# First weight chunk in two halves on one queue, dummy products ahead of the first transposes, and products that wait for half of a transposed tile

## The chip, the cores and the metric

The kernel runs on one core of one Trainium2 chip. The metric is device time in microseconds (us) of one execution: the median over several runs. The core has a matrix engine (TensorE, PE in the profile; its weight loads are listed apart as PEld), VectorE (DVE), ScalarE (ACT), GpSimd (POOL) and SyncE (SP). SP and ACT each have a queue on which they issue transfers between the chip's main memory and the core's on-chip memory; matrix products land in eight banks of an accumulator memory, from which ScalarE and VectorE copy them.

## The reference

One sequence of 256 tokens, model width 1024, all in 32-bit floating point, goes through two kinds of block:

```python
# first_block, two layers
proj = x @ ab_w_in[0]                       # 1024 -> 2840
o    = concat([nsa_attention(...), moba_attention(...)])
x    = layer_norm(ALPHA * x + o @ ab_w_out[0], ...)
x    = layer_norm(ALPHA * x + grouped_moe(x, ...), ...)
q, k, v = split(x @ sb_w_in[0])             # the second mixer
x    = layer_norm(ALPHA * x + mixer(q, k, v) @ sb_w_out[0], ...)
x    = layer_norm(ALPHA * x + grouped_moe(x, ...), ...)
# second_block, one layer
u    = rmsnorm(x) ; proj = u @ w_in_2[0]    # 1024 -> 3104
x    = x + concat([gla_mixer(...), dilated_mixer(...)]) @ w_out_2[0]
u    = rmsnorm(x) ; x = x + hier_moe(u, ...)
out  = rmsnorm(x)
```

The names of the mixers are shortened here; each starts with a projection of the whole normalised input, and each mixture of experts (MoE) starts with a router, a narrow product of the same input.

## The kernel before

The 256 tokens are two tiles of 128 (T = 2), the width of 1024 is eight steps of 128 (KT = 8). Products need the tokens along the free dimension, so ahead of every projection and every router the input is transposed by TensorE into four banks: bank 2t holds steps 0 to 3 of tile t, bank 2t + 1 steps 4 to 7. ScalarE copies banks 0, 1 and 2 into `XT` (L1574, semaphore `xt_act`), VectorE bank 3 (L1884, `xt_dve`). This happens six times, k = 0 to 5: k = 0 for x itself, k = 1, 3 and 5 ahead of the three routers, k = 2 ahead of the second mixer's projection, k = 4 ahead of the second block's.

All the code is written out by hand for each engine; each engine works through its own list in order, and semaphores tie them together. `transpose_x` (L728) issues the transposes of tile 0, then, where it is given, the work `then(0)` behind a wait for both copies of tile 0, then the transposes of tile 1, the filler `between`, and `then(1)` behind a wait for both copies of tile 1. The first call (L904) has no `then`: the products of chunk 0 follow it. The waits for tile t of the normalised input (`normed`) stand ahead of its transposes; VectorE computes the two tiles one after the other.

Weights come in chunks of 2 MB (1024 x 512) into six slots. A chunk's load is issued by SP when TensorE has finished with the chunk six places before it (`chunk_done`); TensorE waits for `slot_loaded`. `project` (L761) multiplies a chunk with both tiles, 16 products of 128x128 by 128x512; each is two instructions in the profile. The first chunk is loaded in two halves of the contraction, steps 0 to 3 by SP (L655) behind x, and steps 4 to 7 by ACT (L1561) behind the first 80 KB of constants, among which is the identity matrix that transposes need; both halves count on the semaphore of slot 0. The small loads of ACT's queue (positions, two small weights, two tables of position embeddings) stand behind its half, and the 1.5 MB of further constants (L1605) behind ScalarE's copies of the first transposes.

`keep_clock_up` (L746) issues products whose results nobody reads, to fill waiting time of TensorE. In the MoEs, `logits` (L1033) is the `then` of `transpose_x`; it is the router's product, and behind it VectorE chooses the experts. The first chunk of the second mixer is `N_SB`, at L1347; the first chunk of the second block `N_2`, at L1426. In both, `then(t)` is `project` for one tile.

## Time and profile before

| | before |
|---|---|
| time, median of 3 runs | 1242.79 us (1242.15 to 1244.42) |
| the profiled execution | 1239.27 us, its span 1237.4 us |
| TensorE busy | 93% of the span |
| TensorE's weight loads, VectorE, ScalarE | 46%, 26%, 17% |
| loaded and stored | 364.41 MB, mean 295 GB/s |

The profile is one execution, recorded by the hardware. Times in it are counted from the span's start. Matrix instructions are pipelined, so the end of a group of them is some 0.2 us after the time at which the next may start.

### The profile page before, as it was taken

How to read it: one execution, taken by the hardware profiler on the slowest of the kernel's cores; microseconds unless marked ns; L12 is line 12 of the kernel's file. 1: busy time of each engine (PE TensorE's matmuls, PEld its weight loads, DVE VectorE, ACT ScalarE, POOL GpSimd, SP SyncE). 2: the span in 40 equal slices, each digit the busy share in tenths (PEclk: the TensorE clock that was granted, in tenths of full speed). 3: DMA queues.
4: the chain of work that ended last, by engine and by line, in shares of the span. 5: the costliest groups of instructions: out<-in, count | busy, mean ns of one | idle time of the engine just before them, and what ended most of it. 6: DMA issues, size and time to landing. Idle time of an engine off the chain costs nothing.

```text
span 1237.4 us, 14481 instructions
## 1 busy us (share of the span) xinstructions
PE 1155.5 (93%) x5884; PEld 565.1 (46%) x5884; DVE 316.2 (26%) x898; ACT 207.6 (17%) x474; POOL 1.0 (0%) x6
## 2 busy tenths in 40 slices
PE   7999999999999999999899999989987998989995
PEld 3555555554687546554364545422422242233231
DVE  1466362112113343111513665100010010000002
ACT  2135321111024412111113231100000000000001
POOL 0000000000000000000000000000000000000000
PEclk9999999999999999999999999999999999999998
DMA  9794135999833133999763244799999999999994
GB/s 311 166 266 180 69 136 243 405 417 390 311 137 136 69 136 130 406 418 389 274 221 136 72 151 186 281 427 426 428 427 429 427 426 430 428 429 426 429 426 185
DMA packets 78250, 364.41 MB, mean 295 GB/s; under 512 B 21458, under 2 KB 26868, under 8 KB 53620
## 3 DMA queue, kind: packets, MB, share of 16 engines
q1 hardware_dynamic: 76724, 360.88, 74.0%
q10 hardware_dynamic: 1472, 2.78, 0.6%
q8 instruction: 38, 0.62, 0.2%
q14 instruction: 16, 0.13, 0.0%
HBM read 362.60 MB, written 1.05 MB: 294 GB/s over the span
## 4 chain that ended last, share of the span: by engine, by line
PE 75%; DMA 15%; DVE 6%; issue 2%; ACT 1%; SPq 0%; ACTq 0%; DVEq 0%
PE bank L1139 17%; DMA weights<-in_expert_w_down_dram 14%; PE bank L1195 9%; PE bank L797 8%; PE bank L819 7%; PE bank L1177 5%; PE bank L769 5%; PE bank L784 4%; PE bank L1232 3%; PE bank L1084 2%; PE bank L809 2%; PE bank L1087 2%; PE bank L847 1%; PE bank L887 1%; PE bank L1372 1%
## 5 line engine op out<-in xcount | busy, mean ns | idle before, releaser
L1139 PE MATMUL bank<-weights,projected 128*64 128x256 f32 (+1 forms) x2048 | 341.1, 489 | 17.3 <-DMA weights<-in_expert_w_up_dram 6.6
L1139 PEld LDWEIGHTS bank<-weights,projected 128*64 128x64 f32 (+1 forms) x2048 | 133.3, 124 | 209.7 <-issue 169.2
L1195 PE MATMUL bank<-weights,work 128*32 128x512 f32 x448 | 106.8, 632 | 23.4 <-DMA weights<-in_expert_w_down_dram 23.4
L797 PE MATMUL bank<-weights,x_transposed 128*128 128x512 f32 x256 | 118.6, 602 | 0.9 <-ACT heads_transposed L1629 0.9
L819 PE MATMUL bank<-weights,mixed 128*128 128x512 f32 x192 | 86.9, 599 | 1.6 <-DVE mixed L2086 1.1
L1195 PEld LDWEIGHTS bank<-weights,work 128*32 128x32 f32 x448 | 30.1, 115 | 97.7 <-issue 97.7
L769 PE MATMUL bank<-weights,x_transposed 128*128 128x512 f32 (+1 forms) x160 | 64.0, 557 | 4.8 <-ACT x_transposed L1574 3.3
L2278 DVE COPY work<-bank 64x512 f32<-64x512 f32 (+1 forms) x30 | 20.7, 689 | 184.8 <-PE bank L1195 125.3
L797 PEld LDWEIGHTS bank<-weights,x_transposed 128*128 128x128 f32 x256 | 45.7, 190 | 47.3 <-issue 45.4
L2298 DVE TENSOR_TENSOR work<-work,bank 64x512 f32<-64x512 f32 (+1 forms) x24 | 16.4, 682 | 199.0 <-PE bank L1139 199.0
L1715 ACT ACTIVATE work<-bank 128x512 f32<-128x512 f32 (+1 forms) x32 | 19.0, 594 | 250.1 <-PE bank L1195 177.7
L1232 PE MATMUL bank<-work,heads_transposed 128*128 128x512 f32 x120 | 59.9, 620 | 0.0
L1177 PE MATMUL bank<-weights,work 128*32 128x512 f32 x512 | 59.9, 597 | 0.0
L819 PEld LDWEIGHTS bank<-weights,mixed 128*128 128x128 f32 x192 | 34.9, 190 | 41.9 <-issue 39.2
L769 PEld LDWEIGHTS bank<-weights,x_transposed 128*128 128x128 f32 x160 | 29.9, 190 | 35.5 <-issue 30.1
L784 PE MATMUL bank<-x_transposed,weights 128*128 128x256 f32 (+1 forms) x208 | 45.7, 380 | 0.0
L784 PEld LDWEIGHTS bank<-x_transposed,weights 128*128 128x128 f32 (+1 forms) x208 | 38.0, 184 | 8.3 <-issue 2.0
L2283 DVE COPY work<-bank 128x256 f32<-128x256 f32 (+1 forms) x24 | 12.2, 510 | 109.1 <-PE bank L1153 109.1
L1725 ACT ACTIVATE work<-bank 64x512 f32<-64x512 f32 (+1 forms) x24 | 14.1, 589 | 150.4 <-PE bank L1139 150.4
L1232 PEld LDWEIGHTS bank<-work,heads_transposed 128*128 128x128 f32 x120 | 19.7, 188 | 40.5 <-issue 36.0
L1084 PE MATMUL bank<-heads_transposed,projected 128*128 128x128 f32 x256 | 31.9, 279 | 0.0
L1084 PEld LDWEIGHTS bank<-heads_transposed,projected 128*128 128x128 f32 x256 | 30.0, 192 | 4.0 <-issue 3.9
(315 smaller groups left out, 983.6 us busy)
## 6 DMA issues: line engine op xcount, KB each, us to landing
weights<-in_expert_w_gate_dram SPq DMA_DIRECT2D x32, 2048.0 KB, 15.7
weights<-in_expert_w_up_dram SPq DMA_DIRECT2D x30, 2048.0 KB, 16.7
weights<-in_expert_w_down_dram SPq DMA_DIRECT2D x30, 2048.0 KB, 17.3
weights<-in_moe_w_gate_dram SPq DMA_DIRECT2D x16, 2048.0 KB, 11.3
weights<-in_moe_w_up_dram SPq DMA_DIRECT2D x16, 2048.0 KB, 12.9
weights<-in_moe_w_down_dram SPq DMA_DIRECT2D x16, 2048.0 KB, 9.5
weights<-in_sb_w_in_dram SPq DMA_DIRECT2D x6, 2048.0 KB, 19.2
weights<-in_w_in_dram SPq DMA_DIRECT2D x6, 2048.0 KB, 14.9
```

Source lines behind the costliest of these rows:

```text
L769: i = mm(BANK[4 + 2 * (seq % 2) + t][:, 0:ncols], XT[:, kt, t * P:(t + 1) * P], w[:, kt, :], start=kt == 0, stop=kt == KT - 1)
L784: i = mm(BANK[4 + 2 * (seq % 2) + c // 2][0:width, (c % 2) * S:(c % 2 + 1) * S], w[:, kt, c * width:(c + 1) * width], XT[:, kt, :], start= ...
L797: i = mm(BANK[6 + t][:, :], XT[:, kt, t * P:(t + 1) * P], w[:, kt, :], start=kt == 0, stop=kt == KT - 1)
L809: i = mm(BANK[6 + half][:, c * S:(c + 1) * S], w[:, kt, (2 * half + c) * P:(2 * half + c + 1) * P], XT[:, kt, :], start=kt == 0, stop=kt = ...
L819: i = mm(BANK[bank][:, :], mixT[:, kt, t * P:(t + 1) * P], w[:, kt, :], start=kt == 0, stop=kt == KT - 1)
L1084: i = mm(to.rearrange("p (q t s) -> p q t s", t=T, s=cap)[:, :, t, :], XP[:, t, kt, :], place.rearrange("p (q s) -> p q s", s=cap), start= ...
L1087: i = mm(to, XP[:, t, kt, :], place, start=t == 0, stop=t == T - 1)
L1139: i = mm(b[n_slots * c:n_slots * (c + 1), e * F:(e + 1) * F], x[:, kt, q * n_slots:(q + 1) * n_slots], w[c][:, col:col + F], start=kt == 0 ...
L1177: i = mm(BANK[2 + half][cap * q:cap * (q + 1), :], hT[:, e * step + f, s0:s0 + cap], slot(n + c)[:, col:col + CH], start=f == 0, stop=f == ...
L1195: i = mm(BANK[2 + half][r0 + n_slots * c:r0 + n_slots * (c + 1), :], hT[:, a * step + f, n_slots * c:n_slots * (c + 1)], extra_weights(c, ...
L1232: i = mm(BANK[4 + 2 * t + half][:, :], w, YS[:, block % 2, half, :], start=False, stop=last and (SPLIT[L] or final))
L2278: cp(YS[r0:r0 + rows, (pair // 2 if rows < P else pair) % 2, 1, :], BANK[3][from0:from0 + rows, :]).then_inc(y1_ready, 1)
```

## The change

The edit has four parts. The second half of chunk 0 moves from ACT's queue to SP's, right behind the first half, and the first half has a semaphore of its own; `project_in_halves` does steps 0 to 3 for both tiles, then steps 4 to 7 for both. Ten products of 128x128 by 128x128, with the identity as both operands and results that nobody reads, stand ahead of the first transposes; they wait for the first constants only. `xt_copied` splits the waits for copies: steps 0 to 3 wait for the first copy of the tile, steps 4 to 7 for the second; the routers and all first projections use it. And `project_first` takes the place of `transpose_x` with `project` for N_SB and N_2: it issues the transposes of tile 1 ahead of the product numbered `second_at`, which is the seventh of tile 0 for N_SB and the first of tile 1 for N_2.

```diff
 def loaded_value(n):
     v = 16 * (n // NSLOT + 1)
-    if n % NSLOT == 0:
-        v += 16
...
-            sp.dma_start(first_chunk_part(0)[0], first_chunk_part(0)[1]).then_inc(slot_loaded[0], 16)
+            sp.dma_start(first_chunk_part(0)[0], first_chunk_part(0)[1]).then_inc(first_half_loaded, 16)
+            sp.dma_start(first_chunk_part(1)[0], first_chunk_part(1)[1]).then_inc(slot_loaded[0], 16)
...
+            def transpose_tile(src, t):
+                for kt in range(KT):
+                    i = nc.tensor.transpose(BANK[2 * t + kt // 4][:, (kt % 4) * P:(kt % 4 + 1) * P], src[:, t, kt, :], ident)
+                    if kt % 4 == 3:
+                        i.then_inc(xt_psum, 1)
+
+            def xt_copied(k, t, kt):
+                if kt == 0:
+                    pe.wait_ge(xt_act, 3 * k + 2 * t + 1)
+                elif kt == 4 and t == 0:
+                    pe.wait_ge(xt_act, 3 * k + 2)
+                elif kt == 4:
+                    pe.wait_ge(xt_dve, k + 1)
+
+            def transpose_x(k, src, waits, then, between):
                 for t in range(T):
                     waits(t)
...
-                    if t < T - 1 and then:
-                        pe.wait_ge(xt_act, 3 * k + 2)
-                        then(t)
-                if between:
-                    between()
-                pe.wait_ge(xt_act, 3 * k + 3)
-                pe.wait_ge(xt_dve, k + 1)
-                if then:
-                    then(T - 1)
+                    transpose_tile(src, t)
+                    if t == 0:
+                        then(0)
+                between()
+                then(1)
...
+            def project_first(n, seq, k, src, second_at):
+                pe.wait_ge(proj_copied, seq - 1)
+                pe.wait_ge(normed, tile_no(NORM_OF_XT[k], 0))
+                transpose_tile(src, 0)
+                chunk_loaded(n)
+                w = slot(n).rearrange("p (k c) -> p k c", k=KT)
+                for t in range(T):
+                    for kt in range(KT):
+                        if t * KT + kt == second_at:
+                            pe.wait_ge(normed, tile_no(NORM_OF_XT[k], 1))
+                            transpose_tile(src, 1)
+                        xt_copied(k, t, kt)
+                        i = mm(BANK[4 + 2 * (seq % 2) + t][:, :], XT[:, kt, t * P:(t + 1) * P], w[:, kt, :], start=kt == 0, stop=kt == KT - 1)
+                i.then_inc(chunk_done, 1)
...
             pe.wait_ge(first_consts_loaded, 16)
-            transpose_x(0, by_k(X), lambda t: pe.wait_ge(x_loaded, 16 * T) if t == 0 else None)
+            for _ in range(10):
+                mm(BANK[7][:, 0:P], ident, ident, start=True, stop=True)
+            pe.wait_ge(x_loaded, 16 * T)
+            for t in range(T):
+                transpose_tile(by_k(X), t)
...
-            project(0, 512, 0)
+            def project_in_halves():
+                w = slot(0).rearrange("p (k c) -> p k c", k=KT)
+                for h in range(2):
+                    if h == 0:
+                        pe.wait_ge(first_half_loaded, 16)
+                    else:
+                        chunk_loaded(0)
+                    for t in range(T):
+                        for kt in range(4 * h, 4 * h + 4):
+                            xt_copied(0, t, kt)
+                            i = mm(BANK[4 + t][:, :], XT[:, kt, t * P:(t + 1) * P], w[:, kt, :], start=kt == 0, stop=kt == KT - 1)
+                i.then_inc(chunk_done, 1)
+
+            project_in_halves()
             project(1, 512, 1)
...
                 def logits(t):
                     for kt in range(KT):
+                        xt_copied(k, t, kt)
...
-            transpose_x(2, by_k(X), lambda t: pe.wait_ge(normed, tile_no(NORM_OF_XT[2], t)),
-                        lambda t: project(N_SB, CH, 6, tiles=(t,)))
+            project_first(N_SB, 6, 2, by_k(X), KT - 2)
...
-            transpose_x(4, by_k(U), lambda t: pe.wait_ge(normed, tile_no(NORM_OF_XT[4], t)),
-                        lambda t: project(N_2, CH, 12, tiles=(t,)))
+            project_first(N_2, 12, 4, by_k(U), KT)
...
-            act.dma_start(first_chunk_part(1)[0], first_chunk_part(1)[1]).then_inc(slot_loaded[0], 16)
```

## Rows read from the trace of the kernel before

**Rows 1.** The page: the chain that ended last, share of the span by engine.

```profile
PE 75%; DMA 15%; DVE 6%; issue 2%; ACT 1%; SPq 0%; ACTq 0%; DVEq 0%
```

**Rows 2.** Stretches (start:end, length, busy by engine, PEclk, DMA share, GB/s).

```profile
765.00:775.00 10.00, 8.75 (x54) 5.92 (x54) 6.27 (x33) 2.08 (x3) 0.00 (x0) 1.00 0.03 13
817.00:1210.00 393.00, 353.39 (x1534) 118.26 (x1536) 31.57 (x52) 22.27 (x37) 0.00 (x0) 0.98 1.01 428
```

**Rows 3.** TensorE's waits: who waited for whom, total us, times, longest.

```profile
PE bank L769 <- ACT x_transposed L1574: 3.3, 4, 0.9
PE bank L1035 <- ACT x_transposed L1574: 2.2, 3, 0.7
```

**Rows 4.** Timeline of the start: start, length, engine, line, operation, idle before.

```profile
0.75 0.41 ACTq L1560 DMA_DIRECT2D consts<-constants_dram  x1
2.12 6.01 SPq L543 DMA_DIRECT2D weights<-in_ab_w_in_dram  x2
6.59 3.65 PE L733 MATMUL bank<-consts,residual 128*128 128x128 f32 x16 [6.59 <-DMA residual<-in_x_dram]
11.77 27.71 PE L769 MATMUL bank<-weights,x_transposed 128*128 128x512 f32 x64 [1.53 <-DMA weights<-in_ab_w_in_dram]
```

**Rows 5.** Transfers issued in the first 15 us: size of each, us to landing.

```profile
weights<-in_ab_w_in_dram SPq DMA_DIRECT2D x1, 2048.0 KB, 19.5
weights<-in_ab_w_in_dram SPq DMA_DIRECT2D x1, 1024.0 KB, 10.0
consts<-constants_dram ACTq DMA_DIRECT2D x1, 80.0 KB, 4.3
```

**Rows 6.** Stretches of the start, columns as in rows 2.

```profile
0.00:5.00 5.00, 0.00 (x0) 0.00 (x0) 0.00 (x0) 0.16 (x1) 0.73 (x5) 1.00 0.58 194
5.00:6.50 1.50, 0.00 (x0) 0.00 (x0) 0.00 (x0) 1.13 (x1) 0.00 (x0) 1.00 1.03 400
```

**Rows 7.** The chain in order of time, a stretch of products of 128 columns.

```profile
184.63 3.98 PE bank L1084 x32
```

**Rows 8.** The transposes (L733): ns min/median/max, first and last start; the start, then all.

```profile
L733 PE MATMUL bank<-consts,residual x16: 417/417/449, 6.6 to 9.8; 128*128 128x128 f32 x16
L733 PE MATMUL bank<-consts,residual x64: 272/276/449, 6.6 to 461.7; 128*128 128x128 f32 x64
```

**Rows 9.** Timeline ahead of the first router.

```profile
174.87 0.60 ACT L1574 ACTIVATE x_transposed<-bank 128x512 f32<-128x512 f32 x1 [3.62 <-PE bank L733]
175.12 1.02 PE L749 MATMUL bank<-consts 128*128 128x512 f32 x2
175.39 0.69 DVE L1884 COPY x_transposed<-bank 128x512 f32<-128x512 f32 x1 [1.32 <-PE bank L733]
176.23 1.93 PE L1035 MATMUL bank<-small_params,x_transposed 128*128 128x20 f32 x16
```

**Rows 10.** Timeline and transfers around N_SB's products.

```profile
297.44 6.74 SPq L543 DMA_DIRECT2D weights<-in_sb_w_in_dram  x1
DMA to landing us min/median/max: 13.8/19.2/21.1
310.72 1.08 ACT L1574 ACTIVATE x_transposed<-bank 128x512 f32<-128x512 f32 x2 [2.96 <-PE bank L733]
313.80 1.28 DVE L1919 SCALAR_TENSOR_TENSOR residual<-residual,misc,norm_params 128x1024 f32<-128x1024 f32 x1
318.82 1.05 PE L733 MATMUL bank<-consts,residual 128*128 128x128 f32 x8
320.77 7.11 PE L769 MATMUL bank<-weights,x_transposed 128*128 128x512 f32 x16 [0.90 <-ACT x_transposed L1574]
```

**Rows 11.** Timeline of N_2's second tile.

```profile
610.76 1.16 PE L733 MATMUL bank<-consts,mixed 128*128 128x128 f32 x8 [0.73 <-DVE mixed L1927]
611.51 0.60 ACT L1574 ACTIVATE x_transposed<-bank 128x512 f32<-128x512 f32 x1 [2.96 <-PE bank L733]
612.82 7.11 PE L769 MATMUL bank<-weights,x_transposed 128*128 128x512 f32 x16 [0.90 <-ACT x_transposed L1574]
```

More of the change, by code:

```diff
@@ L292, in build @@
         x_loaded = sem("x_loaded")
+        first_half_loaded = sem("first_half_loaded")
         first_consts_loaded = sem("first_consts_loaded")
@@ L726, in by_k @@
                 return x.rearrange("p t (c k) -> p t k c", k=KT)
-            def transpose_x(k, src, waits, then=None, between=None):
+            def transpose_tile(src, t):
[11 more added lines that the diff above has]
+            def transpose_x(k, src, waits, then, between):
                 for t in range(T):
                     waits(t)
-                    for kt in range(KT):
-                        i = nc.tensor.transpose(BANK[2 * t + kt // 4][:, (kt % 4) * P:(kt % 4 + 1) * P], src[:, t, kt, :], ident)
-                        if kt % 4 == 3:
-                            i.then_inc(xt_psum, 1)
-                    if t < T - 1 and then:
-                        pe.wait_ge(xt_act, 3 * k + 2)
-                        then(t)
-                if between:
-                    between()
-                pe.wait_ge(xt_act, 3 * k + 3)
-                pe.wait_ge(xt_dve, k + 1)
-                if then:
-                    then(T - 1)
+                    transpose_tile(src, t)
[3 more added lines that the diff above has]
+                then(1)
             def keep_clock_up(n, bank):
@@ L759, in _, with project @@
                 HALF_FREE[N_2 + 3 + c, 1] = (proj_copied, 15 + c) if c else (proj_copied, 14)
-            def project(n, ncols, seq, between=None, tiles=range(T)):
+            def project_first(n, seq, k, src, second_at):
[12 more added lines that the diff above has]
+                i.then_inc(chunk_done, 1)
+            def project(n, ncols, seq):
                 if seq >= 2:
@@ L766, in project @@
                 w = slot(n)[:, 0:KT * ncols].rearrange("p (k c) -> p k c", k=KT)
-                for t in tiles:
+                for t in range(T):
                     for kt in range(KT):
@@ L770, in project @@
                                start=kt == 0, stop=kt == KT - 1)
-                    if t == 0 and between:
-                        between()
-                if t == T - 1:
-                    i.then_inc(chunk_done, 1)
+                i.then_inc(chunk_done, 1)
             def project_T(n, seq, tiles, width=P, between=None):
@@ L912, in tr @@
                 i.then_inc(qt_psum, 1)
-            project(0, 512, 0)
+            def project_in_halves():
[5 more added lines that the diff above has]
+                        chunk_loaded(0)
+                    for t in range(T):
+                        for kt in range(4 * h, 4 * h + 4):
+                            xt_copied(0, t, kt)
+                            i = mm(BANK[4 + t][:, :], XT[:, kt, t * P:(t + 1) * P], w[:, kt, :], start=kt == 0, stop=kt == KT - 1)
+                i.then_inc(chunk_done, 1)
+            project_in_halves()
             project(1, 512, 1)
```

## The prediction

> **What bounds the kernel now.** I read the chain that ended last first, then the waits of TensorE, and only then the stages that the change touches. TensorE holds 75% of the chain, transfers 15% [rows 1]. So a microsecond counts if it is taken from TensorE's own queue, or from a wait at its head, in a stretch where TensorE is what everyone else waits for. The transfer part of the chain lies in the third MoE: from 817 to 1210 us the queues move 428 GB/s without a pause, while just before, from 765 to 775 us, they are nearly idle at 13 GB/s [rows 2]. That long stream begins when the first unit of this MoE has used its weights, so it starts when TensorE gets there: its length is fixed, its start is not. What is won anywhere before it should therefore reach the end.
>
> TensorE's waits in the touched stages are few and short: 6.6 us for x, 1.5 us for the first weights [rows 4], and copies of transposed tiles, 3.3 us ahead of the products and 2.2 us ahead of the router's [rows 3]. These are all that the change can take, 13.6 us in name; the question is what lies right behind each.
>
> **The first stage.** TensorE starts at 6.59 us, when x has landed; it makes 16 transposes until 10.2 us, waits, and starts the products at 11.77 us, when chunk 0 has landed (SP's half took 10.0 us from its issue, just ahead of chunk 1's at 2.12 us) [rows 4, 5]. After that the products of chunks 0 and 1 run without a gap, 64 half-products in 27.71 us, 0.433 us each, so 0.86 us a product and 13.85 us a chunk [rows 4]. So all that counts here is when the first product starts and that no later one waits.
>
> Transfers: in the first 5 us 0.97 MB are moved (194 GB/s), then 400 GB/s [rows 6]. With x alone on SP's queue and only the 80 KB of constants ahead on ACT's, x (1.05 MB) is in at about 5.4 us instead of 6.5, half one at (2.18 - 0.97) / 0.4 = 3.0 us after 5.0, so 8.0 us, half two at about 10.7 us. The small loads of ACT's queue no longer stand behind the half chunk and now run beside x; even 1 us more for that leaves 9.0 and 11.7 us.
>
> The Trainium skill (DMA: Bandwidth & Descriptors, "Issuing engines are not separate DMA queues") says that loads from SP and ACT run on the same 16 engines and interleave, and a second issuer saves only issue time. By it the move costs no bandwidth and only reorders; no row here has the start of the kernel on one queue, but the long stream of the last MoE, nearly all of it on SP's queue, agrees with its 428 GB/s.
>
> But x is no longer what TensorE waits for. The ten dummies wait for the first constants, which land at 0.75 + 4.3 = 5.05 us [rows 4, 5], and the transposes stand behind them in TensorE's queue. A product of this shape (128 columns, two instructions) takes 0.249 us at the upper level of the clock (32 instructions in 3.98 us) [rows 7]. The first 16 transposes take 417 ns each and 3.65 us in all; the other transposes take 276 ns, and eight of them 1.05 us with the end of the last one, 0.11 us apart [rows 4, 8, 10]. The start thus runs at the lower level, 1.2 GHz, by these durations, though the granted clock in the row reads 1.00 [rows 6]; the products after 1.5 us of idle time are at the upper one. Ten dummies therefore cost 4.3 us at the lower level (20 instructions of 0.215 us, the spacing of those first transposes) or 2.5 us at the upper, and the 16 transposes 3.4 or 1.8 us. Both bounds: the first product at 5.1 + 4.3 + 3.4 = 12.8 us (1.0 us lost), or at 5.1 + 2.5 + 1.8 = 9.4 us (2.4 us won). I take dummies at the lower and transposes at the upper level, because in the row of before a like amount of work at the lower level is followed by the upper one: 5.1 + 4.3 + 1.8 = 11.2 us, **0.6 us won**. The first copy (0.6 us after the fourth transpose) is ready by then, half one has landed long before. Half two is wanted 6.9 us after the start, at 18 us. Chunk 1 landed at 2.12 + 19.5 = 21.6 us and would be wanted at 25.0 us [rows 5]; the big constants, issued by ACT behind its copies, come about 2 us later and are wanted only far behind. SP issues one load more ahead of chunk 1 and all behind it, 0.43 us of its time, ACT one less; neither is near the end of a wait. Using the first chunk half by half is costed at nothing: with the dummies ahead, its landing is not what decides.
>
> **The three routers.** The logits of tile 0 can start half a copy (0.5 us) earlier, but behind them TensorE waits for the second normalised tile anyway, so nothing. For tile 1 the order is: transposes, ScalarE's copy at 174.87 to 175.47, VectorE's at 175.39 to 176.08, a filler product at 175.12 that holds TensorE until 175.12 + 2 x 0.43 = 175.98, the logits at 176.23 [rows 9]. With the wait split, the first four may start behind the filler, and the other four (0.5 us later) find VectorE's copy done. That is 0.25 us, and VectorE takes the logits at once. The bounds are 0.1 and 0.3 us; three MoEs: **0.75 us won**.
>
> **The first projection of the second mixer (N_SB).** Before: products of tile 0 behind two copies, 310.72 + 1.08 = 311.8; transposes of tile 1 at 318.82; products of tile 1 only at 320.77, behind the copies, until 327.88 [rows 10]. After: the first copy is ready at 310.72 + 0.60 = 311.32, the products start 0.45 us earlier, at 311.38. The transposes of tile 1 come after six products, at 311.38 + 6 x 0.86 = 316.5; the normalised tile they need is done at 313.80 + 1.28 = 315.08, so nothing waits; the last two products (1.7 us) cover both copies. The work is 16 x 0.86 + 8 x 0.11 = 14.6 us, ending at 326.0 instead of 327.88: **1.85 us won**. Bounds: 1.4, if the copies are not wholly covered, and 2.0. The second chunk, wanted at 326.0, is there: the fourth of the six loads was issued at 297.44 and none took over 21.1 us, so the first four have landed by 318.5 [rows 10].
>
> **The first projection of the second block (N_2).** Here the second transposes stay behind all products of tile 0 and wait for VectorE's normalised tile, at 610.76 in any case, so the earlier start is worth nothing. Behind them, the products of tile 1 start when ScalarE's copy is done, 611.51 + 0.60 + 0.07 = 612.18, instead of at 612.82, behind VectorE's: **0.65 us won**, 0.4 to 0.7 [rows 11]. VectorE's copy is wanted four products later.
>
> **Sum.** 0.6 + 0.75 + 1.85 + 0.65 = 3.85 us. The profiled execution took 1239.27 us, 1237.4 of it span; it would come to 1235.4. The median of the runs shown is 1242.79, 3.5 us above it, and the gain does not hang on that: 1242.79 - 3.85 = 1238.9 us. Its own range is the sum of the bounds: a gain of -1.0 + 0.3 + 1.4 + 0.4 = 1.1 to 2.4 + 0.9 + 2.0 + 0.7 = 6.0 us, 1236.8 to 1241.7.
>
> **Rivals.** (a) The transposes stay at the lower level behind the dummies. Then the first stage loses 1.0 us, the total gain is 2.25 us, 1240.5 us. Speaking for it: nothing in the trace shows a rise of the clock behind products so small. Against: all later transposes run at 272 to 276 ns [rows 8]. The Trainium skill (TensorE: Matmul & The Clock Gate, "Part 4: PE-mode transpose") says that the full clock does not engage for transposes; that would give this rival. The rows with 276 ns against 417 ns disagree.
>
> (b) Gains are given back: a stage behind is held by a transfer, VectorE or ScalarE that did not move. The candidates are the attention behind the first stage, where VectorE and ScalarE alternate with TensorE, and the stretch around 690 to 705 us. Half the gain gone gives 1240.9, all of it 1242.8 us. Against it: those waits hang on TensorE's products and shift along with them.
>
> (c) Slower: one queue is worse than two at the start, and chunk 1 becomes late, since half two now stands ahead of it. It decides from the moment that chunk 1 lands after 25.0 us; to eat the other stages' 3.25 us too and be slower by 2.5 us, it would have to land after 31.3 us. The 5.3 MB up to its end and 1.5 MB of constants would have to move at some 230 GB/s, 6.8 MB in 29.8 us; the first 5 us have such a rate (194 GB/s), the next stretch 400, and before, chunk 1 came at 21.6 us behind the same bytes [rows 5, 6]. Landing at 31.5 us gives 1245.4 us.
>
> (d) The clock is up early, or the dummies are cheap: the first stage wins 1.6 to 2.4 us, 1237.9 to 1237.1 us.
>
> **Chances.** Forecast 60%, (d) 10%, (a) 12%, (b) 13%, (c) 5%. About 0.2% (2.5 us) is what a measurement of this kernel can tell from no change. The forecast and (d) are faster by more than that: 70%; (a) and (b) within it: 25%; (c) slower: 5%. The range 1236.9 to 1241.9 leaves out (c), the worse half of (b) and the edges.
>
> **What would show it.** In the profile after: dummies from about 5.1 us and the first product between 10.8 and 11.7 us, whatever the landing of half one; transposes of about 276 ns behind the dummies (417 ns is rival a); no idle time of TensorE ahead of the second half or of chunk 1 (else c); the logits of tile 1 starting 0.86 us after the filler instead of 1.11; the second mixer's first chunk taking 14.6 us instead of 16.1 from its first product; tile 1 of N_2 starting 1.4 us after its transposes instead of 2.1; and the start of the third MoE's long transfer stream, which lies between 775 and 817 us now [rows 2], about 3.8 us earlier. If that start has moved and the end has not, the transfer stream was not tied to it and the forecast is wrong.

## The result, and the profile of the kernel after

The changed kernel takes 1235.65 us (median of 4 runs, 1235.25 to 1236.14), the kernel before 1243.12 us in the same comparison (4 runs, 1242.15 to 1244.42): a ratio of 0.9939, interval 0.9923 to 0.9954. Forecast were 1238.9 us with a range of 1236.9 to 1241.9. The sign is right; the time lies below the range, and the gain is larger than the 3.85 us of the sum. Two later comparisons on other chips give 0.9956 and 0.9957 (5.1 and 5.7 us), so the first one's 7.5 us is the largest of three; all three are above 3.85.

The profiled execution after took 1236.14 us, 1234.4 of it span, against a span of 1237.4 before. So between the two profiled executions only 3.0 us were won. The difference between these 3.0 us and the 5.1 to 7.5 us of the medians is what had to be explained.

The page after, its span and its chain of waits:

```profile
span 1234.4 us, 14516 instructions
PE 74%; DMA 17%; DVE 6%; issue 1%; ACT 1%; SPq 0%; ACTq 0%; DVEq 0%
```

The timeline of the start after, to set beside [rows 4], then the instructions of the dummies (L926) and of the first transposes (L731), min/median/max ns, then the stretch of [rows 6] from 5.0 to 6.5 us:

```profile
5.24 3.92 PE L926 MATMUL bank<-consts 128*128 128x128 f32 x20 [5.24 <-DMA consts<-constants_dram]
8.99 1.94 PE L731 MATMUL bank<-consts,residual 128*128 128x128 f32 x16
10.77 13.90 PE L950 MATMUL bank<-weights,x_transposed 128*128 128x512 f32 x32
24.51 13.90 PE L793 MATMUL bank<-weights,x_transposed 128*128 128x512 f32 x32
L926 PE MATMUL bank<-consts x20: 275/421/583, 5.2 to 8.9; 128*128 128x128 f32 x20
L731 PE MATMUL bank<-consts,residual x16: 272/274/276, 9.0 to 10.7; 128*128 128x128 f32 x16
5.00:6.50 1.50, 1.26 (x6) 1.26 (x7) 0.00 (x0) 0.81 (x1) 0.00 (x0) 1.00 0.70 221
```

The transposes stand directly behind the dummies and run at 274 ns instead of 417 [rows 8]. The first product comes at 10.77 us, 1.00 us earlier. Chunk 0 (L950) and chunk 1 (L793) follow each other without a gap.

The two halves of chunk 0, issued at L654 and L655, and their times from issue to landing:

```profile
L654 SPq DMA_DIRECT2D weights<-in_ab_w_in_dram x1: 433/433/433, 1.7 to 1.7; - x1
DMA to landing us min/median/max: 8.6/8.6/8.6
L655 SPq DMA_DIRECT2D weights<-in_ab_w_in_dram x1: 731/731/731, 2.1 to 2.1; - x1
DMA to landing us min/median/max: 10.7/10.7/10.7
```

The first half landed at 10.2 us (1.66 + 8.6), the second at 12.9 us (2.13 + 10.7). Before, the later of the two halves landed at 11.6 us. The sum had half one at 8.0 to 9.0 us and half two at 10.7 to 11.7 us.

The first router after (compare [rows 9]), N_SB ([rows 10]) and N_2 ([rows 11]):

```profile
169.76 1.96 PE L1075 MATMUL bank<-small_params,x_transposed 128*128 128x20 f32 x16 [0.24 <-ACT x_transposed L1611]
174.94 1.02 PE L757 MATMUL bank<-consts 128*128 128x512 f32 x2
175.80 1.86 PE L1075 MATMUL bank<-small_params,x_transposed 128*128 128x20 f32 x16
311.04 5.39 PE L782 MATMUL bank<-weights,x_transposed 128*128 128x512 f32 x12 [0.33 <-ACT x_transposed L1611]
316.27 1.05 PE L731 MATMUL bank<-consts,residual 128*128 128x128 f32 x8
317.15 8.75 PE L782 MATMUL bank<-weights,x_transposed 128*128 128x512 f32 x20
325.74 2.54 PE L805 MATMUL bank<-x_transposed,weights 128*128 128x256 f32 x11
608.47 1.16 PE L731 MATMUL bank<-consts,mixed 128*128 128x128 f32 x8 [1.09 <-DVE mixed L1964]
609.87 5.42 PE L782 MATMUL bank<-weights,x_transposed 128*128 128x512 f32 x12 [0.24 <-ACT x_transposed L1611]
```

N_SB's first product before, and what followed its last one:

```profile
311.85 7.13 PE L769 MATMUL bank<-weights,x_transposed 128*128 128x512 f32 x16 [0.73 <-ACT x_transposed L1574]
327.71 2.54 PE L784 MATMUL bank<-x_transposed,weights 128*128 128x256 f32 x11
```

Each touched stage comes near what the sum said. Tile 1's logits start 0.86 us behind the filler (175.80 - 174.94) instead of 1.11. N_SB's chunk lasts 14.70 us from its first product to what follows (325.74 - 311.04) instead of 15.86 (327.71 - 311.85), and nothing idles ahead of the second transposes. N_2's second tile starts 1.40 us after its transposes (609.87 - 608.47) instead of 2.06. The third MoE then begins 3.26 us earlier, and its transfer stream is as fast as before [rows 2]. From the chain in order of time, before and after, and the stretch of the kernel after:

```profile
774.47 7.06 PE bank L1139 x32
771.21 7.06 PE bank L1179 x32
817.00:1210.00 393.00, 354.27 (x1534) 118.22 (x1532) 31.07 (x51) 22.28 (x37) 0.00 (x0) 0.97 1.01 428
```

One gain was given back on the way. The lead of 1.00 us at the first product is 1.07 us behind chunk 2, and 0.17 us at the first router. In between, in the attention, the granted clock falls for some 3.4 us in this execution, while products run (the stretch's columns as in [rows 2]):

```profile
80.00:81.00 1.00, 1.00 (x3) 0.43 (x2) 0.93 (x4) 0.00 (x0) 0.00 (x0) 0.50 1.01 371
82.00:83.00 1.00, 1.00 (x2) 0.33 (x2) 0.96 (x6) 0.86 (x5) 0.00 (x0) 0.50 1.08 207
```

Of all 20 traces of this case, 13 have such a fall in the attention: near 80 us, for 0.9 us of time, in 4, and between 104 and 108 us, for 0.5 us, in 9. With the old start it is in 4 of 6 traces, with the new one in 9 of 14, so no clear difference between the kernels is seen in it, though the one near 80 us is in none of the six; and the first profile of the kernel before has none and that of the kernel after has the dearer one.

### The profile page after: what moved, and what is told of

The parts are those of the page before. It is cut to its first block, busy times and chain, and to the rows that moved or that the text cites. A ratio compares the mean times of both kernels' runs of the same rounds, so it can differ in the third digit from the quotient of the medians.

```text
span 1234.4 us, 14516 instructions
## 1 busy us (share of the span) xinstructions
PE 1158.1 (94%) x5904; PEld 568.3 (46%) x5904; DVE 316.1 (26%) x898; ACT 207.6 (17%) x474; POOL 1.0 (0%) x6
## 4 chain that ended last, share of the span: by engine, by line
PE 74%; DMA 17%; DVE 6%; issue 1%; ACT 1%; SPq 0%; ACTq 0%; DVEq 0%
DMA weights<-in_expert_w_down_dram 16%; PE bank L1179 16%; PE bank L1235 9%; PE bank L818 9%; PE bank L840 7%; PE bank L1217 5%; PE bank L805 4%; PE bank L1272 3%; PE bank L1124 2%; PE bank L830 2%; PE bank L1127 2%; PE bank L793 2%; PE bank L782 2%; PE bank L868 1%; PE bank L950 1%
## 5 line engine op out<-in xcount | busy, mean ns | idle before, releaser
L818 PE MATMUL bank<-weights,x_transposed 128*128 128x512 f32 x256 | 120.3, 609 | 0.9 <-ACT heads_transposed L1666 0.9
L1235 PEld LDWEIGHTS bank<-weights,work 128*32 128x32 f32 x448 | 30.7, 116 | 98.6 <-issue 98.6
L2315 DVE COPY work<-bank 64x512 f32<-64x512 f32 (+1 forms) x30 | 20.7, 690 | 186.3 <-PE bank L1235 126.7
L818 PEld LDWEIGHTS bank<-weights,x_transposed 128*128 128x128 f32 x256 | 46.1, 192 | 47.9 <-issue 46.0
L2320 DVE COPY work<-bank 128x256 f32<-128x256 f32 (+1 forms) x24 | 12.2, 510 | 106.9 <-PE bank L1193 106.9
L1217 PEld LDWEIGHTS bank<-weights,work 128*32 128x32 f32 x512 | 14.2, 109 | 38.3 <-issue 36.1
L782 PE MATMUL bank<-weights,x_transposed 128*128 128x512 f32 x64 | 28.4, 596 | 0.9 <-ACT x_transposed L1611 0.9
## 6 DMA issues: line engine op xcount, KB each, us to landing
weights<-in_moe_w_up_dram SPq DMA_DIRECT2D x16, 2048.0 KB, 12.8
```

The costliest lines, as they stand in the source:

```text
L782: i = mm(BANK[4 + 2 * (seq % 2) + t][:, :], XT[:, kt, t * P:(t + 1) * P], w[:, kt, :], start=kt == 0, stop=kt == KT - 1)
L818: i = mm(BANK[6 + t][:, :], XT[:, kt, t * P:(t + 1) * P], w[:, kt, :], start=kt == 0, stop=kt == KT - 1)
L1217: i = mm(BANK[2 + half][cap * q:cap * (q + 1), :], hT[:, e * step + f, s0:s0 + cap], slot(n + c)[:, col:col + CH], start=f == 0, stop=f == ...
L1235: i = mm(BANK[2 + half][r0 + n_slots * c:r0 + n_slots * (c + 1), :], hT[:, a * step + f, n_slots * c:n_slots * (c + 1)], extra_weights(c, ...
```

## The experiments

The ratios are to the kernel before, timed beside the kernel on the same chip; kernels compared with each other across comparisons ran on different chips. "Undone" means: the changed kernel with that part as before.

### The kernel before again

Two theories were open for the missing 2 us or more: a part of the change is worth more than its term, or the profiled execution of before lacks losses that a typical one has. First the kernel before, unchanged, was measured and profiled again, to see whether the execution of [rows 1 to 11] stands for its median.

> The kernel before, unchanged, for more of its executions and a second trace. The change won 7.5 us between the medians but only 3.0 us between the two profiled spans, because the profiled execution of before (1239.3 us) is 3.9 us shorter than the median of the others. Theory A (the clock): ordinary executions of before run part of the time with TensorE at its lower level, at places where the profiled one did not; then this trace shows one or more stretches with a granted clock of 0.5, of some 3.5 us each, and the executions scatter by 2 to 5 us. Theory B (transfers): the stream of the last MoE takes another length from one execution to the next; then the clock is 1.00 up to 800 us here too, and the difference lies behind 817 us. Theory C: the profiled execution was an odd one for no reason that a trace shows, and all times here lie within 1242 to 1244.5 us with a trace like the first.

Measured: 1241.31 us (12 runs, 1239.05 to 1243.03), ratio 1.0001 (0.9992 to 1.0011). The new profiled execution has a span of 1241.1 us, 3.7 us more than the first, with the same program. Its timeline shows where. First the start, and the half-products that begin from 12 to 14 us, in this run's trace ahead of the first profile's:

```profile
12.15 28.34 PE L769 MATMUL bank<-weights,x_transposed 128*128 128x512 f32 x62 [1.44 <-DMA weights<-in_ab_w_in_dram]
L769 PE MATMUL bank<-weights,x_transposed x3: 1061/1061/1193, 12.2 to 14.0; 128*128 128x512 f32 x3
L769 PE MATMUL bank<-weights,x_transposed x6: 592/592/667, 11.8 to 14.0; 128*128 128x512 f32 x6
```

The first products last 1061 ns instead of 592. From the first product to the first small product behind chunk 2 it takes 46.16 us here and 44.67 in the first profile: 1.5 us. Then the first router, timeline and stretches:

```profile
172.80 1.96 PE L1035 MATMUL bank<-small_params,x_transposed 128*128 128x20 f32 x16 [0.73 <-ACT x_transposed L1574]
175.50:176.00 0.50, 0.50 (x2) 0.29 (x1) 0.50 (x1) 0.00 (x0) 0.00 (x0) 0.60 1.08 459
176.00:176.50 0.50, 0.50 (x2) 0.01 (x1) 0.43 (x1) 0.00 (x0) 0.00 (x0) 0.50 1.04 442
178.50:179.00 0.50, 0.50 (x4) 0.50 (x4) 0.00 (x0) 0.50 (x2) 0.00 (x0) 0.50 0.04 16
179.00:179.50 0.50, 0.50 (x3) 0.16 (x2) 0.27 (x1) 0.50 (x1) 0.00 (x0) 0.99 0.08 33
```

The granted clock is 0.50, TensorE at 1.2 GHz instead of 2.4, from about 175.6 to 179.0 us, behind the wait for the copies and the small logits. From the router's first transposes to the MoE's first products it takes 22.48 us (171.03 to 193.51) against 21.02 in the first profile. With the first product 0.38 us later and a fall of 0.5 us in the attention that makes 3.8 us, and the third MoE begins 3.80 us later here. So the first profile was an execution without any of these losses. The theory that the last MoE's transfers differ is out: from the third MoE's first product to the end it takes 462.9 us in both, and 461.7 to 463.5 us in all 20 traces, of every kernel.

### The start

Old start, the rest changed (run twice, on two chips):

```diff
-            for _ in range(10):
-                mm(BANK[7][:, 0:P], ident, ident, start=True, stop=True)
...
+            pe.wait_ge(xt_act, 3)
+            pe.wait_ge(xt_dve, 1)
...
-            project_in_halves()
+            project(0, 512, 0)
```

The loads of the first chunk are those of before, too.

> The changed kernel with the start of before: half of the first chunk on ScalarE's queue, no dummies, the first products behind all four copies. Kept: routers, first projections of the second mixer and of the second block. If the stages add up as forecast (0.75 + 1.85 + 0.65 us), it is 3.25 us faster than before, about 1239.9 us. If the 4 us above the forecast come from the start (a rival), it stays near 3 us and the changed kernel is 4 to 4.5 us faster than this one. If they come from behind the start, it is 6 us or more faster than before.

> Once more the changed kernel with the start of before, since six executions were few: 1236.15 us then, against 1236.09 of the changed kernel in another job. The traces put the first small products behind chunk 2 at 58.3 and 58.5 us (old start) or 56.4 (the first profile), and at 55.4 to 57.3 us with the new start, on the mean 1.3 us apart. If that reaches the end, this one is 1 to 1.4 us slower than the changed kernel (about 4 us faster than before); if the attention behind it gives it back, within 0.4 us of it (5 us faster than before).

Measured: 1236.15 us, 0.9964 (0.9950 to 0.9978), and 1237.36 us, 0.9960 (0.9945 to 0.9974). Against 0.9957 for the whole change, measured in another comparison, the start is worth 0.4 to 0.9 us, less than the intervals' width. The reverse, the new start alone on the kernel before:

> Only the start of the changed kernel (half chunks on one queue, ten dummies, halves used one by one); routers and first projections as before. Forecast: 0.6 us faster than before. In the trace of the changed kernel the first product comes 1.0 us earlier, but a stretch at the lower clock at 80 us takes 0.8 us of it back. If the start has the missing 4 us, this is 4 to 5 us faster, about 1238.5 us; if not, it is 0 to 1 us faster.

Measured: 1240.40 us, 0.9993 (0.9979 to 1.0007), 0.9 us and not told apart from nothing. Then the dummies alone were left out (run twice):

```diff
-            for _ in range(10):
-                mm(BANK[7][:, 0:P], ident, ident, start=True, stop=True)
```

> The changed kernel without the ten dummies. If TensorE's queue is what decides the start, the transposes start when x lands, about 6.6 us, at the lower level (3.4 us), and the first product at about 10.1 to 10.5 us instead of 10.77: 0.3 to 0.7 us faster than the changed kernel. If the dummies are what brings the clock up in time, the first products run at the lower level for a while (each us of it costs 0.5 us) and it is 0.5 to 2 us slower. If the clock's phase set at the start decides later stretches too, the difference is larger than what the start shows.

> The changed kernel without the ten dummies, a second time: in its first trace the products started at 10.35 us, 0.4 us earlier than with dummies, but then took 0.85 us more, as if the first 1.7 us of them were at the lower clock. With the first result (1236.03 us) I expect no difference from the changed kernel of more than 0.5 us either way. If dummies are what the start gains by, it is 1 us slower.

Measured: 1236.03 us, 0.9960 (0.9948 to 0.9973), and 1235.20 us, 0.9952 (0.9938 to 0.9967), where the changed kernel beside the second has 1235.62 us, 0.9957. The dummies bring nothing to the time that these runs can tell. The first product comes earlier without them:

```profile
10.35 10.04 PE L948 MATMUL bank<-weights,x_transposed 128*128 128x512 f32 x21 [0.19 <-DMA weights<-in_ab_w_in_dram]
```

Without dummies the landing of half one does end the wait. What the traces show of the start, all together: with the old start the products up to chunk 2 took 46.2 to 46.6 us in 4 of 6 traces and 44.7 in the others, from a first product at 11.8 to 12.2 us; with dummies 44.6 us in all 12, from a first product at 10.8 to 12.7 us, 11.6 on average; without dummies 44.7 and 45.5 us from 10.3 us. The first router is reached at 170.3, 168.8 and 168.1 us on average. So the new start avoids a loss of 1.5 to 1.9 us that the old one has in part of its executions, and apart from that it is only some 0.3 us earlier at the first product; the first product at 10.77 us in the profile after is the earliest of the twelve. Which part of the new start avoids the loss is not shown: no run undid the halves or the one queue alone.

### N_SB and N_2

Each undone by itself: the transposes of tile 1 behind all of tile 0's products, and each tile's products behind both copies.

```diff
-            project_first(N_SB, 6, 2, by_k(X), KT - 2)
+            project_first_old(N_SB, 6, 2, by_k(X))
...
-            project_first(N_2, 12, 4, by_k(U), KT)
+            project_first_old(N_2, 12, 4, by_k(U))
```

> The changed kernel with the second mixer's first projection as before: the transposes of tile 1 behind all products of tile 0, products behind both copies. By the shortened stage alone it is 1.6 to 1.85 us slower than the changed kernel; if the idle time around it (1.7 us ahead of and between the products) also lets the clock fall in part of the executions, 3 to 4 us slower.

> The changed kernel with the second block's first projection as before: products behind both copies of a tile. By the shortened stage alone it is 0.65 us slower than the changed kernel; if the clock falls there in part of the executions, 1.5 to 2.5 us slower.

Beside them the changed kernel itself:

> The changed kernel, unchanged, for its time beside the three kernels sent with it and a second trace. In the runs so far, the kernel with the old start (1236.15 us) is 5.3 us faster than before (1241.4), not 3.25, and the changed kernel 7.5 us. Theory A: 3.2 us of the gain are the shortened stages themselves, which the traces show one by one (0.2 to 0.35 us a router, 1.6 us the second mixer's first projection, 0.7 us the second block's), and the rest is that before spends, in most executions, one or two stretches of 3.4 us at the lower clock in critical places where the changed kernel has them less often. Then this one is 5.5 to 7.5 us faster than before in this job too, and its trace shows no low stretch at a router. Rival: the rest is the scatter of the medians; then it is within 1 us of 3.9 us faster.

Measured: the changed kernel 1236.09 us, 0.9956 (0.9944 to 0.9968); N_SB undone 1237.81 us, 0.9969 (0.9957 to 0.9981); N_2 undone 1236.72 us, 0.9962 (0.9950 to 0.9973). So N_SB is worth 1.7 us (forecast 1.85) and N_2 0.6 us (forecast 0.65), each near its forecast. With six runs of each, N_2's 0.6 us is within their scatter; the traces show it (2.06 against 1.40 us above).

### The routers

```diff
                 def logits(t):
+                    xt_copied(k, t, 0)
+                    xt_copied(k, t, 4)
                     for kt in range(KT):
-                        xt_copied(k, t, kt)
```

> The changed kernel with the routers of before: the logits wait for both copies of a tile. By the shortened stages alone it is 0.75 us slower than the changed kernel. If the routers' idle time is what lets the clock fall there (theory A, as in the second trace of before, with a low stretch from 174 to 180 us that costs 1.4 us), it is 2 to 3 us slower, and its trace may show a low stretch in one of the three routers.

Measured: 1238.74 us (12 runs, 1236.74 to 1240.05), 0.9976 (0.9964 to 0.9987). This part alone is worth 2.65 us beside the changed kernel of the same comparison, where 0.75 was forecast. The 12 runs lie in three clusters, around 1237.2, 1238.6 and 1239.8 us, some 1.3 us apart, as if something that costs this much happened in none, one or two places (12 later runs of this kernel have no such clusters). Its trace has one fall of the clock, at the second router (timeline and a stretch):

```profile
456.14 1.93 PE L1076 MATMUL bank<-small_params,x_transposed 128*128 128x20 f32 x16 [0.81 <-ACT x_transposed L1612]
457.92 1.68 PE L1085 MATMUL bank<-residual,consts 128*128 128x512 f32 x2
458.50:459.00 0.50, 0.50 (x2) 0.34 (x1) 0.50 (x1) 0.00 (x0) 0.00 (x0) 0.50 0.89 377
```

The new theory: at full clock the split is worth about the 0.75 us that was computed; the rest is a fall of the clock which the idle 0.7 to 0.9 us ahead of tile 0's logits brings about in some visits to a router. The rival: the split itself saves more than the rows show. They are told apart by a filler, a product that nobody reads, in the idle time: it fills the idle time and leaves the wait as it is. Old routers with the filler, and the split of one tile alone:

```diff
+                    if t == 0:
+                        keep_clock_up(1, 3)
                     xt_copied(k, t, 0)
                     xt_copied(k, t, 4)
```

> The changed kernel with the routers of before, and one filler product more (128x128 by 128x512, 0.86 us) between the transposes of tile 0 and the logits of tile 0, in a free bank, where TensorE otherwise waits 0.8 to 0.9 us for copies. The old routers cost 2.65 us (1238.74 against 1236.09), not 0.75. If 1.9 us of that are falls of the clock behind that wait, the filler wins them back although it only adds work: 0.75 us slower than the changed kernel, 4.3 us faster than before (ratio about 0.9965). If the waits themselves cost the time, it is as slow as the old routers: 2.4 us faster than before (0.998).

> The changed kernel with the split waits in the routers for tile 0 only; tile 1 waits for both copies. I valued the split of tile 0 at nothing and that of tile 1 at 0.25 us a router. If the clock falls behind the wait ahead of the logits of tile 0, nearly the whole 2.65 us come from tile 0: this one is 0.75 us slower than the changed kernel (about 4.3 us faster than before). If not, it is as slow as the old routers, 2.4 us faster than before.

> The counterpart: the split for tile 1 only. By the clock theory it keeps the 0.75 us of tile 1 and loses the 1.9 us of tile 0: 1.9 us slower than the changed kernel, 3.2 us faster than before (0.9974). By the waits alone it would equal the changed kernel, 5.1 us faster than before.

Measured: filler 1236.87 us, 0.9959 (0.9946 to 0.9972); tile 0 split 1236.67 us, 0.9955 (0.9940 to 0.9970); tile 1 split 1238.37 us, 0.9974 (0.9961 to 0.9988). All three were timed in one comparison: the filler and tile 0's split both keep the gain, tile 1's doesn't. The traces give the mechanism. Timelines of the first router and stretches there, first with tile 1's split alone, then with tile 0's:

```profile
168.57 1.05 PE L731 MATMUL bank<-consts,residual 128*128 128x128 f32 x8
170.45 2.06 PE L1079 MATMUL bank<-small_params,x_transposed 128*128 128x20 f32 x16 [0.82 <-ACT x_transposed L1615]
172.34 2.06 PE L1088 MATMUL bank<-residual,consts 128*128 128x512 f32 x2
174.18 1.69 PE L757 MATMUL bank<-consts 128*128 128x512 f32 x2
175.71 1.05 PE L731 MATMUL bank<-consts,residual 128*128 128x128 f32 x8
172.00:173.00 1.00, 1.00 (x5) 0.81 (x5) 0.86 (x5) 0.00 (x0) 0.00 (x0) 0.55 1.04 442
173.00:174.00 1.00, 1.00 (x2) 0.34 (x1) 0.98 (x1) 0.00 (x0) 0.00 (x0) 0.50 1.00 426
```

```profile
169.86 1.96 PE L1079 MATMUL bank<-small_params,x_transposed 128*128 128x20 f32 x16 [0.24 <-ACT x_transposed L1615]
171.66 1.10 PE L1088 MATMUL bank<-residual,consts 128*128 128x512 f32 x2
174.03 1.17 PE L731 MATMUL bank<-consts,residual 128*128 128x128 f32 x8 [0.41 <-DVE residual L1960]
172.00:174.00 2.00, 1.63 (x4) 0.38 (x2) 1.84 (x5) 0.00 (x0) 0.00 (x0) 1.00 0.99 418
```

With the wait of 0.82 us the pair of products at L1088 takes 2.06 us instead of 1.10 and the fillers 1.69 instead of 1.02; the transposes of tile 1 come 7.14 us after tile 0's (175.71 - 168.57). In the kernel after they come at 173.94, 5.46 us after those at 168.48. In this trace a second fall of the same kind stands at the second router. Counted over the traces, the fall appears in 6 of 18 router visits with tile 0's old wait (six traces, all six falls at the first or second router) and in none of 42 with its split or a filler (14 traces). Each lasts about 3.4 us. All of them begin 1.6 to 2.8 us behind the start of tile 0's small logits.

What each part is worth at full clock can be read from the same traces. From a router's first transposes to the first product of its MoE's experts it takes 21.0 us with the old waits (21.35 at the third router), the same with a filler and the same with tile 0's split alone, so that split is worth nothing at full clock; with both splits it takes 20.7 us (21.0), so tile 1's split is worth 0.32 to 0.34 us, of which 0.2 to 0.35 remain at the next stage. With a fall it takes 22.5 to 22.6 us with the old waits, and 22.25 instead of 20.7 with tile 1's split: a fall costs 1.5 us.

The old routers once more, on another chip, beside the routers' split alone on the kernel before:

> The changed kernel with the routers of before, a second time, beside e17 in one job: 3.15 us faster than before by the means of the first job. If the split's value were 2.7 us everywhere, e17 and this one together (2.7 + 3.15) give the whole 5.7 us; if this comes out at 4 us or more, the first result was high by scatter and the routers' share smaller.

> The kernel before with the split waits in the three routers and nothing else of the change. Taken away from the changed kernel, the split costs 2.7 us; a filler in the routers' wait won that back there, but in the kernel before it won only 0.8 to 1.1 us. If the parts add up, this is 2.7 us faster than before; if falls of the clock at the routers are rarer in before than in the kernel with the other parts of the change, it is 1.5 us faster: 0.75 us of shortened stages and 0.8 us of clock.

Measured: routers undone 1239.71 us, 0.9981 (0.9970 to 0.9992), two falls in its trace; routers alone 1240.10 us, 0.9989 (0.9977 to 1.0001), no fall at the routers. By the ratios undoing costs 3.0 us ((0.9981 - 0.9957) x 1241), but the split alone on the kernel before wins 1.2 us by the medians and 1.9 by the means, and its interval reaches to no gain. The filler in the kernel before, without any split:

```diff
+                    if t < T - 1 and between:
+                        keep_clock_up(1, 3)
                     if t < T - 1 and then:
```

> The kernel before with nothing but one filler product (0.86 us) in each of the three routers, between the transposes and the logits of tile 0, where TensorE waits 0.7 to 0.8 us for copies. The filler is 0.1 us longer than the wait, so by the work alone this is 0 to 0.3 us slower than before. If the clock's falls behind that wait are what the forecast missed, it is some 2 us faster than before (the filler won 1.9 us on top of the changed kernel with old routers): ratio about 0.9985.

Measured: 1240.25 us, 0.9994 (0.9985 to 1.0003), 0.8 us by the means and not told apart from nothing: no fall in its trace at the routers, but less than the 1.9 us that the filler restored in the changed kernel. The means of both comparisons allow for it if falls are rarer in the kernel before than in the changed one with old routers (1 of 9 visits against 5 of 9 in the traces, that with tile 1's split alone among the latter), but nine visits each don't settle that. Nor is "old routers" quite the wait of before: two waits in a row stand there for one, and TensorE idles 0.82 us where the kernel before idles 0.73.

### More fillers, and the changed kernel a third time

One trace (N_2 undone) had a fall of the clock in N_2 too, behind the same kind of wait but early in a row of large products, so two more fillers were added, one ahead of the transposes of each tile. The fall in the trace with N_2 undone, timeline and a stretch:

```profile
601.60 6.68 PE L782 MATMUL bank<-weights,x_transposed 128*128 128x512 f32 x11 [0.73 <-ACT x_transposed L1627]
602.50:603.00 0.50, 0.50 (x1) 0.05 (x1) 0.43 (x3) 0.00 (x0) 0.00 (x0) 0.50 1.07 393
```

```diff
+                            if second_at == KT:
+                                keep_clock_up(1, 1)
...
-            keep_clock_up(6, 1)
+            keep_clock_up(7, 1)
```

> The changed kernel with two more filler products around the second block's first projection: one more ahead of the transposes of tile 0 (seven instead of six) and one ahead of the transposes of tile 1, where TensorE waits 1.1 us each for VectorE. One trace (old second block's projection) has a fall of the clock there, at 602 us. If such falls happen in some executions of the changed kernel too, this one is 0.2 to 0.7 us faster than it; if the short wait that the change left (0.33 us) never lets the clock fall, they are the same.

> The changed kernel once more, for a direct comparison in this job: 5 to 7.5 us faster than before, within 1235 to 1237 us.

Measured: with the fillers 1236.10 us, 0.9960 (0.9946 to 0.9973), without 1235.62 us, 0.9957 (0.9942 to 0.9971). No gain that these runs can tell, and no fall in N_2 in either trace. No version tried is clearly faster than the changed kernel.

## Why the prediction was wrong in its size

**The sum, against its own profiled execution, came out within 1 us.** 1239.27 - 3.85 gives 1235.4 us; the profiled execution after took 1236.14, and the medians of the changed kernel are 1235.65, 1236.09 and 1235.62. By stages of the two profiles: the start 1.07 us for 0.6, the routers 0.8 for 0.75, N_SB 1.6 for 1.85, N_2 0.7 for 0.65, together 4.2; less the 0.9 us of the fall in the attention, the third MoE begins 3.26 us earlier for 3.8. In part that is luck: the start did better in this execution than in most, and the fall took nearly as much away. N_SB's term was a little too large because it set the end of the last product before (327.88) against a sum of starts; what followed started at 327.71. That the lead at the third MoE reaches the end is borne out by the constant rest of 461.7 to 463.5 us in all traces.

**The step that failed is "The median of the runs shown is 1242.79, 3.5 us above it, and the gain does not hang on that".** It does. The kernel before scatters from 1238.6 to 1246.8 us over the 35 runs of one comparison; the changed kernel in two comparisons, 12 runs, from 1234.7 to 1237.0. The 3.5 us are in part losses that other executions of the kernel before have and the profiled one had not, and the change takes some of them away. Two of these were found: slow first products (1.5 to 1.9 us, in 4 of 6 traces with the old start, 0 of 12 with the new one), and falls of the clock at the routers (1.5 us each, 6 of 18 visits against 0 of 42). How often a typical execution of the kernel before has them is known from few traces only.

**Within the sum, the term of tile 0's logits was wrong**: "behind them TensorE waits for the second normalised tile anyway, so nothing". At full clock that is right (21.0 us with or without this split), and it is how a wait is read on a timeline. But without the 0.7 to 0.9 us of idle time ahead of the small products the falls did not come, as the filler shows, which fills the gap and leaves the wait, and restores 1.9 us. The routers' part was sized at 0.75 us; taking it out of the changed kernel cost 2.65 and 3.0, putting it alone into the kernel before won 1.2 to 1.9.

**The start's term (0.6 us) was about right in size and wrong in what it is made of.** In the two profiles 1.00 us is won at the first product, over all traces 0.3 us on average; in the times 0.4 to 0.9 us. Rival (a) is refuted: the transposes run at 272 to 276 ns behind the dummies, in the other traces with dummies 274 to 278 by their median, though some of the first still take up to 421. The Trainium skill (TensorE: Matmul & The Clock Gate, "Part 4: PE-mode transpose") says that the full clock doesn't engage for them; the rows disagree. Rival (d), dummies cheap or the clock up early, came true in part: the dummies took 3.75 us from the first to the transposes (8.99 - 5.24), between the two bounds of 2.5 and 4.3, and their last ones took 275 ns for the 421 of most, so the clock rose near their end. But the dummies are no source of the gain.

**"Using the first chunk half by half is costed at nothing" was wrong too**, and nothing in the forecast time shows it. The sum had all of chunk 0 landed by 11.7 us at the latest; on one queue it landed at 12.9 us, 1.2 us later than before, and from 12.8 to 13.2 us in all 14 traces with the new start. Between 5.0 and 6.5 us the transfers moved 221 GB/s where the kernel before moved 400 (181 to 249 against 400 to 406 in all traces), so x landed at 6.3 us and not at 5.4. Without the wait for the first half alone, the first product could not have started before 12.9 us, some 2 us later than it did (an estimate from these landings; no run shows it). And as half one lands only at 10.1 to 10.6 us, a first product at 9.4 us, the upper bound, was out of reach. Whether the one queue or the small loads beside x cost the transfers their speed is not shown.

**Rival (b)** happened in the profiled execution, where all but 0.17 us of the start's gain was gone at the first router; what was named for it, waits of VectorE and ScalarE, was not the cause, but a fall of the clock that both kernels have. **Rival (c)** had its premise in part, chunk 0 being 1.2 us later, but not its effect: chunk 1 took 19.0 us from its issue, 19.5 before, landed at 21.9 us where 24.5 was soon enough, and no product waited.

**The range** took its ends from the bounds of the terms alone. With a scatter of 8 us in the kernel before and a profile at its lower edge, it should have reached to 1239.27 - 3.85 = 1235.4 us and below; a range that spans the sum laid against either baseline, 1235.4 and 1238.9 us, has the measured time just inside.

**Open.** The parts don't add up in the same way from both ends. Taken out one at a time they are worth 0.4 to 0.9 (start), 2.65 to 3.0 (routers), 1.7 and 0.6, together 5.4 to 6.2 us, which agrees with the 5.1 to 5.7 of the whole. Put in alone, the routers bring 1.2 to 1.9 and the start 0.9. Why falls should be rarer in the kernel before, and why one execution of a program has a fall where another has none, is not known. And how much of the first comparison's 7.5 us is its small number of runs was not settled; the kernel before alone differs by 2 us between comparisons (1241.15 to 1243.12), the changed one by 0.5.

## What to carry to other kernels

Ahead of an estimate against a profile, ask where this one execution lies in the scatter of the runs: if its time is at the fast edge, the losses that make the median are not in its rows, and a second profile of the same program can show them. A short wait on TensorE ahead of tiny products can cost more than its length when the clock falls behind it, so a wait is not costless because a later one would absorb it; a split wait or a single filler product in the gap is a cheap trial. And when a transfer is moved to another queue, look up where each piece landed: a median over two pieces hides that one came early and the other late.

## What was not expected of the hardware

- TensorE's clock fell to granted 0.50 (1.2 GHz) for about 3.4 us behind an idle stretch of only 0.7 to 0.9 us followed by sixteen products of 20 columns, in 6 of 18 cases, in an engine that was otherwise busy; once it fell behind waits of 0.97 and 0.73 us, early in a row of products of 512 columns (N_2 undone). The Trainium skill (TensorE: Matmul & The Clock Gate, "Why this matters for your kernels") warns of long idle gaps between bursts of matmuls. No such long gap stands ahead of these falls, so the traces go beyond that advice: here gaps of 0.7 to 0.9 us were enough, and without them there was no fall at a router.
- At the start the granted clock of the stretches reads 1.00 while products last 1061 ns and not 592. The durations, not that column, tell the level there.
- With the halves of chunk 0 on one queue and the small loads beside x, the transfers moved 181 to 249 GB/s between 5.0 and 6.5 us in 14 traces, and 400 to 406 in the six with the old start.
- Ten dummy products ahead of the transposes bring these from 417 to 274 ns each and leave the time where it was (1235.20 us without, 1235.62 with).
